# Latent attention by pairs of heads over four score banks, banded values projected features first, inner key products in 64x64 tiles

## The chip, the cores and the metric

The kernel runs on one core of one Trainium2 chip. The metric is the device time of one execution in microseconds (us). Three runs of the kernel before gave a median of 1982.02 us (1980.81 to 1982.16). The work is written out by hand for each engine: TensorE (PE, with its weight loads as PEld), VectorE (DVE), ScalarE (ACT), GpSimd (POOL) and the DMA queue of SyncE (SP), tied together with semaphores.

## What is computed

Three transformer layers over 512 tokens of width 1024, all in float32. Layer 1 ("even") has eight stick-breaking heads and eight banded heads (a window of 128 keys, two key heads), layer 2 ("mla") latent attention, layer 3 ("mix2") a linear recurrence (RWKV-7) beside differential attention. A feed-forward block follows each. The change touches these parts:

```python
# banded heads: k_b, v_b are 128 columns each of h @ w_in
# latent attention, 16 heads, 64 + 32 query/key features, 64 value features
s = (einsum('bhqd,bshd->bhqs', qn, k_nope) + einsum('bhqr,bsr->bhqs', qr, k_rope)) * 96 ** -0.5
s = where(key_pos <= q_pos, s, -inf)
p = softmax(s, axis=-1)
out = einsum('bhqs,bshd->bqhd', p, v)            # then @ w_o
# recurrence: state = state * w + (state @ -kk) (kk * a)^T + v k^T, here in chunks of 64 tokens;
# within a chunk it needs, for each head, the 64x64 products of (kk * a) with kk
```

## The kernel before

Activations lie features first: `X[:, k, :]` is 128 features by 512 tokens. A product with a weight is three products, of high and low parts (`XH`, `XL`, `w_hi`, `w_lo`) in fp32r; small products (scores, values, transposes) are plain f32, and an f32 product appears in the trace as two instructions. Weights come in units of up to 2048 columns; SP loads them, ACT makes the high part and DVE the low part (`split`), and PE waits for it (`unit`). Eight banks of PSUM hold results, and `linear`, `feature_tile` and `token_tile` (line 2365) go round banks 0 to 3.

**Banded values** (`even`, lines 2643 to 2656). After the key product of the last input unit (one `feature_tile`, line 2340, 24 products of 512 columns) PE computes the values tokens first, in four token tiles of 24 products of 128 columns each (line 2365), each waiting until DVE has emptied the bank before (line 1771). Then PE waits for the last of them (`lin_free`) and enters `stick_breaking`: `z(2)` (line 2523), then for each head `suffix(h)` (2538, 2543), `values(h-1)` (2554) and `z(h+2)`. `suffix(h)` waits for DVE's `two_parts(h)` (1668, 1670), which DVE does between the value tiles for head 1. ACT's `ln_part(h)` waits for `z(h)`.

**Latent attention** (`attention("mla0")`, `attention("mla1")`). Eight heads in each half, and 24 groups: for each head, query block 3 with 4 key tiles (512 columns), block 2 with 3 (384), and blocks 0 and 1 with 1 and 2 (384). Score banks are 0 to 2. On PE the order is `scores(n+2)` (2415, mask product 2418), `turn(n)` (2431, one transpose for each key tile), `values(n-1)` (2445: a tile of turned weights, 128x128, is stationary, and 64 value columns move past it). DVE takes the row maxima (1555) and their negation (1558), ACT the exponential with its row sum (1081) and the copy of the turned weights (1070). When a head is done, DVE normalises its output (`head_end`, 1570 and 1582) into `otok_m`, tokens first. In the second half `turn_pair` (2802, four transposes) turns two heads' output back to features first, ACT takes the high part (1295) and DVE the low part (1991). The output projection `mla_out` (2393, then 2340) starts after the eighth pair's turn.

**Inner key products** (`inner`, line 2957, within the last two units of `diff_in`). For each of four tiles `t` of two heads, ACT copies the keys of four chunks at a time as blocks of a 128x128 block-diagonal matrix (`ABD`, which DVE clears at line 2141, copies at line 1409), and PE multiplies each with 64 columns: 8 products (16 instructions) for each `t`. DVE masks the result into `Ak` (2125). PE's order is token tile 0, `inner(0)`, `inner(1)`, token tile 1, `inner(2)`, `inner(3)`, token tiles 2 and 3, and then it waits for all four (`rw_ak`). The inverse of the chunk matrices (SP, POOL) starts from `Ak` and runs beside `attention("diff")`.

```python
                for n in range(N):
                    if n + 2 < N:
                        scores(n + 2)
                    between(n)
                    turn(n)
                    if n >= 1:
                        values(n - 1)
                values(N - 1)
```

Of the kernel before, what the change touches and what calls it, by code (L numbers as in the profile page):

```python
# [8 lines left out]
F32 = mybir.dt.float32  # L9
# [4 lines left out]
ALU = mybir.AluOpType  # L14
AX = mybir.AxisListType

P = 128
# [147 lines left out]
LIN_TILES = {"even": 8 + 8 + 4 + 1 + 4 + 8, "mla": 6 + 2 * (8 + 4 + 4) + 8, "mix2": 8 + 8 + 14 + 8}  # L165


def build(nc, d, out, scratch, stages):
# [18 lines left out]
    with ExitStack() as ctx:  # L187
# [121 lines left out]
        at_p = sem("at_p")  # L309
        at_t = sem("at_t")  # L310
# [45 lines left out]
        abd_zero = sem("abd_zero")  # L356
        rw_abd = sem("rw_abd")
# [49 lines left out]
        PTb = region(2 * 512, 2, 512)  # L407
        base1 = taken[0]
# [38 lines left out]
        otok_m = region(ST * D, ST, D)  # L447
# [41 lines left out]
        ABD = NS.rearrange("p b (a c) -> p b a c", c=P)  # L489
# [76 lines left out]
        for half in range(2):  # L566
            ATT[f"mla{half}"] = dict(groups=causal_groups(), heads=8, dv=64,
                                     q=lambda h: qc[0:96, h, :], k=lambda h: kc[0:96, h, :],
                                     v=lambda h, j: vm[:, j, 64 * h:64 * h + 64], scale=96.0 ** -0.5, mask=True, q_col=True)
        ATT["diff"] = dict(groups=causal_groups(), heads=8, dv=128,  # L570
                           q=lambda h: qd[0:66, h, :], k=lambda h: kd[0:66, h, :],
                           v=lambda h, j: vd[j][:, 128 * (h // 2):128 * (h // 2) + 128], scale=0.125, mask=True, q_col=False)
        att_order = []
        for s in stages:
            att_order += {"mla": ["mla0", "mla1"], "mix2": ["diff"]}.get(s, [])
        gb = hb = 0
        for a in att_order:
            ATT[a]["g0"], ATT[a]["h0"] = gb, hb
            ATT[a]["list"] = [(h, i, tiles) for h in range(8) for i, tiles in enumerate(ATT[a]["groups"])]
            gb += len(ATT[a]["list"])  # L580
            hb += 8
        ot_base = {}
        n_ot = 0
        for s in stages:
            ot_base[s] = n_ot
            n_ot += {"even": 4, "mla": 8, "mix2": 4}.get(s, 0)

# [72 lines left out]
        def units_read():  # L660

            tiles = {"even_qkv": (2, 2, 2, 2, 4, 4), "even_qb": (0, 4), "even_kvb": (5,), "diff_in": (2, 2, 2, 2, 4, 4)}
# [29 lines left out]
        MLA_TURNS = {2: 0, 5: 1, 8: 2, 11: 3, 14: 4, 17: 5, 21: 6}  # L692
# [295 lines left out]
        def _(act):  # L988
# [55 lines left out]
            def turned_kept(k):  # L1044
                act.wait_ge(turned, 9 + k + 1)
# [13 lines left out]
            def attention(name, between=lambda n: None):  # L1059
# [12 lines left out]
                for n, (h, gi, tiles) in enumerate(groups):  # L1072
# [7 lines left out]
                    for i, k0, nk, c in tiles:  # L1080
                        last = act.activation(Pb[:, g % 3, c:c + P * nk], src[:, c:c + P * nk], ACT.Exp,
                                              bias=negm[:, hh % 2, i:i + 1],
                                              scale=qs[:, i:i + 1] if A["q_col"] else A["scale"],
# [213 lines left out]
            def mla():  # L1297
# [18 lines left out]
                for half in range(2):  # L1316
# [25 lines left out]
                    if half == 0:  # L1342
                        attention("mla0")
# [1835 lines left out]
```

## Time and profile before

| | us |
|---|---|
| median of 3 runs | 1982.02 (1980.81 to 1982.16) |
| the profiled execution | 1980.99 |
| its span, first to last instruction | 1979.0 |
| TensorE busy | 1929.9 (98%) |
| VectorE busy | 1003.2 (51%) |
| ScalarE busy | 746.1 (38%) |
| GpSimd busy | 199.8 (10%) |
| chain that ended last, by engine | PE 87%, DVE 8%, ACT 3%, issue 2% |

A TensorE row of a timeline gives the start and length of a run of like instructions. Their lengths hold the time in the pipeline, so that neighbours overlap; what an instruction costs is read from one start to the next. "Stretches" are windows of the span with each engine's busy time in them. The mean granted TensorE clock over the span is 0.993.

### The profile page before, as it was taken

Reading aid. Unit: us, or ns where it says so; the run is one execution under the profiler, and the core shown is the slowest. Engines: PE = TensorE matmul, PEld = TensorE weight load, DVE = VectorE, ACT = ScalarE, POOL = GpSimd, SP = SyncE. Lnnn points to the kernel's source line nnn. Section 1 sums busy time; section 2 is a strip of 40 time slices with the busy share of each in tenths; the row PEclk is TensorE's granted clock in tenths of the full one; section 3 lists DMA queues with packets and bytes.
Section 4 is the critical chain, followed back from the end, with each engine's and each line's share of the span. In section 5 each row is a group of like instructions: output and inputs, shape, how many; then the busy total and the mean of one; then the engine's idle time right before and its main releaser. Section 6 shows DMA issues by size and latency. Waiting matters only on the chain.

```text
span 1979.0 us, 26891 instructions
## 1 busy us (share of the span) xinstructions
PE 1929.9 (98%) x10771; PEld 1575.4 (80%) x10771; DVE 1003.2 (51%) x1349; ACT 746.1 (38%) x1116; POOL 199.8 (10%) x223
## 2 busy tenths in 40 slices
PE   8999999999999999999999999999989999999998
PEld 6886788888888777888888888777879777888887
DVE  6435644333434766543434333758573467665623
ACT  4226532222223564632222222535452444333423
POOL 3000010000000412020000000402371100000001
PEclk9999899999999999999999999999999999999999
DMA  5310022332223111023233222322120223233231
GB/s 169 107 64 1 26 87 89 102 105 86 106 85 98 58 34 64 1 88 106 85 106 95 96 99 92 98 85 64 23 65 4 92 70 105 91 100 106 86 106 64
DMA packets 137778, 158.73 MB, mean 80 GB/s; under 512 B 15960, under 2 KB 125536, under 8 KB 137696
## 3 DMA queue, kind: packets, MB, share of 16 engines
q1 hardware_dynamic: 136256, 155.01, 24.5%
q0 software_dynamic: 1440, 2.58, 0.5%
q8 instruction: 58, 0.95, 0.2%
q14 instruction: 24, 0.20, 0.0%
HBM read 153.89 MB, written 3.68 MB: 80 GB/s over the span
## 4 chain that ended last, share of the span: by engine, by line
PE 87%; DVE 8%; ACT 3%; issue 2%; DMA 0%; POOL 0%; SPq 0%; DVEq 0%; ACTq 0%; POOLq 0%
PE bank L2723 34%; PE bank L2756 16%; PE bank L2340 14%; PE bank L2365 3%; PE bank L2415 3%; PE bank L2445 3%; PE bank L2774 2%; PE bank L2431 1%; DVE XL L1532 1%; DVE w_lo L1525 1%; PE bank L2669 1%; PE bank L2702 1%; PE bank L2523 1%; PE bank L2393 1%; PE bank L2490 1%
## 5 line engine op out<-in xcount | busy, mean ns | idle before, releaser
L2723 PE MATMUL bank<-XH,w_hi 128*128 128x512 f32 x992 | 387.1, 390 | 2.6 <-DVE w_lo L1818 1.9
L2723 PE MATMUL bank<-XH,w_lo 128*128 128x512 f32 x992 | 386.1, 389 | 0.0
L2723 PE MATMUL bank<-XL,w_hi 128*128 128x512 f32 x992 | 386.1, 389 | 0.0
L2723 PEld LDWEIGHTS bank<-XH,w_hi 128*128 128x128 f32 x992 | 186.2, 188 | 42.2 <-DVE w_lo L1818 2.4
L2723 PEld LDWEIGHTS bank<-XL,w_hi 128*128 128x128 f32 x992 | 186.2, 188 | 39.3 <-issue 0.5
L2723 PEld LDWEIGHTS bank<-XH,w_lo 128*128 128x128 f32 x992 | 186.2, 188 | 38.4
L2340 PE MATMUL bank<-XH,w_hi 128*128 128x512 f32 x504 | 200.8, 398 | 4.8 <-DVE w_lo L1525 2.5
L2340 PE MATMUL bank<-XH,w_lo 128*128 128x512 f32 x504 | 197.1, 391 | 0.0
L2340 PE MATMUL bank<-XL,w_hi 128*128 128x512 f32 x504 | 196.9, 391 | 0.0
L1525 DVE TENSOR_TENSOR w_lo<-w_raw,w_hi 128x2048 fp32r<-128x2048 f32 (+4 forms) x65 | 118.1, 1835 | 91.6 <-ACT w_hi L1008 91.2
L1008 ACT ACTIVATE w_hi<-w_raw 128x2048 fp32r<-128x2048 f32 (+5 forms) x66 | 98.3, 1510 | 121.3 <-PE bank L2340 50.0
L1880 DVE TENSOR_TENSOR w_lo<-w_raw,w_hi 128x2048 fp32r<-128x2048 f32 x24 | 55.0, 2292 | 174.3 <-ACT w_hi L1268 174.3
L2756 PE MATMUL bank<-XH,w_hi 128*128 128x512 f32 x320 | 124.6, 389 | 0.0
L2756 PE MATMUL bank<-XH,w_lo 128*128 128x512 f32 x320 | 124.5, 389 | 0.0
L2756 PE MATMUL bank<-XL,w_hi 128*128 128x512 f32 x320 | 124.5, 389 | 0.0
L2340 PEld LDWEIGHTS bank<-XH,w_hi 128*128 128x128 f32 x504 | 95.0, 189 | 30.3 <-DVE w_lo L1525 4.8
L1846 DVE TENSOR_TENSOR arena<-bank,arena 128x512 f32<-128x512 f32 x66 | 45.4, 690 | 141.9 <-PE bank L2723 141.9
L1216 ACT ACTIVATE w_hi<-w_raw 128x2048 fp32r<-128x2048 f32 x32 | 61.3, 1915 | 147.5 <-PE bank L2723 147.5
L1268 ACT ACTIVATE w_hi<-w_raw 128x2048 fp32r<-128x2048 f32 x24 | 46.0, 1917 | 187.1 <-PE bank L2756 166.5
L2340 PEld LDWEIGHTS bank<-XL,w_hi 128*128 128x128 f32 x504 | 95.1, 189 | 20.8 <-issue 1.4
L2340 PEld LDWEIGHTS bank<-XH,w_lo 128*128 128x128 f32 x504 | 95.0, 188 | 19.9
L1824 DVE TENSOR_TENSOR w_lo<-w_raw,w_hi 128x2048 fp32r<-128x2048 f32 x33 | 75.6, 2290 | 62.9 <-ACT w_hi L1234 56.1
(425 smaller groups left out, 3393.6 us busy)
## 6 DMA issues: line engine op xcount, KB each, us to landing
w_raw<-in_ffn_w_gate SPq DMA_DIRECT2D x22, 1024.0 KB, 5.4
w_raw<-in_ffn_w_up SPq DMA_DIRECT2D x22, 1024.0 KB, 5.3
w_raw<-in_ffn_w_down SPq DMA_DIRECT2D x22, 1024.0 KB, 4.9
w_raw<-in_w_up SPq DMA_DIRECT2D x22, 1024.0 KB, 5.0
w_raw<-in_w_in SPq DMA_DIRECT2D x13, 1024.0 KB, 5.3
w_raw<-in_w_down SPq DMA_DIRECT2D x11, 1024.0 KB, 4.9
w_raw<-in_even_w_in SPq DMA_DIRECT2D x9, 1024.0 KB, 5.4
w_raw<-in_even_w_out SPq DMA_DIRECT2D x4, 1024.0 KB, 5.1
```

The costliest lines, as they stand in the source:

```text
L1008: last = act.activation(to, frm, ACT.Copy)
L1216: act.activation(w_hi[:, (u0 + 1) % 2, :], w_raw[:, (u0 + 1) % 2, :], ACT.Copy).then_inc(w_hi_ready, 1)
L1268: act.activation(w_hi[:, slot, :], w_raw[:, slot, :], ACT.Copy).then_inc(w_hi_ready, 1)
L1525: last = dve.tensor_tensor(to, frm, hi.bitcast(F32), ALU.subtract)
L1824: dve.tensor_tensor(w_lo[:, a, :], w_raw[:, a, :], w_hi[:, a, :].bitcast(F32), ALU.subtract).then_inc(w_lo_ready, 1)
L1880: dve.tensor_tensor(w_lo[:, slot, :], w_raw[:, slot, :], w_hi[:, slot, :].bitcast(F32), ALU.subtract).then_inc(w_lo_ready, 1)
L2340: m = pe.matmul(bank[to][0:M, :], cols(w, k), x[:, x0 + k, :], start=(first_k and k == 0 and j == 0), stop=(last_k and k == kt - 1 and j = ...
L2365: m = pe.matmul(bank[to][:, 0:N], x[:, x0 + k, s * P:(s + 1) * P], cols(w, k), start=(k == 0 and j == 0), stop=(k == kt - 1 and j == 2))
L2415: m = pe.matmul(bank[g % 3][:, c:c + P * nk], q(h)[:, P * i:P * (i + 1)], k(h)[:, P * k0:P * (k0 + nk)], start=True, stop=True)
L2445: m = pe.matmul(bank[5 + hh % 2][:, dv * i:dv * (i + 1)], PTb[:, g % 2, c + P * j:c + P * (j + 1)], v(h, k0 + j), start=(j == 0), stop=(j ...
L2723: m = pe.matmul(bank[b][:, :], w[:, k, P * c:P * (c + 1)], x[:, k, :], start=(k == 0 and j == 0), stop=(k == KT - 1 and j == 2))
L2756: m = pe.matmul(bank[p][:, :], left, right, start=False, stop=(stop and c == 1 and j == 2))
```

## The change

Three parts, in one edit.

1. The banded values become one feature tile of 24 products of 512 columns. DVE scales it into `vb` (features first), PE turns it with four transposes after `z(2)`, and DVE copies the result over `vb`. `LIN_TILES` and the counts of `turned` follow.
2. Both latent halves use a new `latent_attention`. Groups run by pairs of heads: block 3 of both, block 2 of both, blocks 0 and 1 of both. Score banks are 0, 1, 2 and 7, and scores run three groups ahead. DVE divides the exponentials by their row sums before the transpose. In the values product the 64 value columns are stationary and 128 turned weights move past, the even head into partitions 0 to 63 of the bank and the odd head into 64 to 127, so that the output comes features first; ACT and DVE make its two parts straight from there. `turn_pair` and `head_end` are gone. The first tile of `mla_out` waits for pairs 6 and 7 only where it reaches them.
3. `inner` takes for each chunk two 64x64 products, one for each head, straight from `aa`; `ABD`, its clearing and ACT's copies are gone.

```diff
@@ PE, even @@
-                for t in range(4):
-                    if t >= 1:
-                        pe.wait_ge(lin_free, L - 1)
-                    token_tile(u, KT, 256, whole(P), P, 0, t, L, to=KVB[(t + 1) % 2]).then_inc(lin_ready, 1)
-                    L += 1
-                pe.wait_ge(lin_free, L)
-                stick_breaking()
+                feature_tile(u, KT, 256, whole(P), P, 0, L, to=KVB[1]).then_inc(lin_ready, 1)
+                L += 1
+                stick_breaking(L)
+            def values_turned(L):
+                pe.wait_ge(lin_free, L)
+                for t in range(ST):
+                    m = pe.transpose(bank[KVB[0]][:, P * t:P * (t + 1)], vb[:, t, :], ident)
+                m.then_inc(turned, 1)
                 z(2)
+                values_turned(L)
@@ DVE, even @@
-                for t in range(4):
-                    dve.wait_ge(lin_ready, L + 1)
-                    dve.tensor_scalar(vb[:, t, :], bank[KVB[(t + 1) % 2]][:, 0:P], rcol[:, t:t + 1], None,
-                                      ALU.mult).then_inc(lin_free, 1)
-                    L += 1
-                    if t == 1:
-                        two_parts(1)
+                dve.wait_ge(lin_ready, L + 1)
+                dve.tensor_tensor(flat, bank[KVB[1]][:, :], rstd, ALU.mult).then_inc(lin_free, 1)
+                L += 1
+                two_parts(1)
+                dve.wait_ge(turned, 10)
+                dve.tensor_copy(flat, bank[KVB[0]][:, :]).then_inc(turned_out, 1)
@@ DVE, latent_attention @@
+                def normalised(n):
+                    dve.wait_ge(at_p, g + 1)
+                    link(dve.reciprocal(rsum[:, h % 2, i0:i1 + 1], rsum[:, h % 2, i0:i1 + 1]))
+                    for i, k0, nk, c in tiles:
+                        w = Pm[:, g % 4, c:c + P * nk]
+                        last = dve.tensor_scalar(w, w, rsum[:, h % 2, i:i + 1], None, ALU.mult)
+                    last.then_inc(at_w, 1)
+                def pair_low(p):
+                    dve.wait_ge(ot_hi, ot_base["mla"] + pp + 1)
+                    dve.tensor_tensor(lo, bank[5 + pp % 2][:, :], hi.bitcast(F32), ALU.subtract).then_inc(ot_lo, 1)
+                for n in range(len(groups)):
+                    maxima(n)
+                    if n >= 1:
+                        normalised(n - 1)
+                    if n % 6 == 5 and n >= 11:
+                        pair_low(n // 6 - 1)
+                normalised(len(groups) - 1)
+                pair_low(3)
@@ ACT, latent_attention: exp(n), then @@
+                    if n >= 2:
+                        evacuate(n - 2)
+                    if n % 6 == 4 and n >= 10:
+                        pair_high(n // 6 - 1)
@@ PE, latent_attention @@
+                def values(n):
+                    pe.wait_ge(at_pt, g + 2)
+                    if gi == 0 and pp >= 2:
+                        pe.wait_ge(ot_lo, ot_base["mla"] + pp - 1)
+                    for i, k0, nk, c in tiles:
+                        for j in range(nk):
+                            for e in range(2):
+                                m = pe.matmul(bank[5 + pp % 2][64 * e:64 * e + 64, P * i:P * (i + 1)],
+                                              vm[:, k0 + j, 64 * (h + e):64 * (h + e) + 64],
+                                              PTm[:, (g + e) % 4, c + P * j:c + P * (j + 1)],
+                                              start=(j == 0), stop=(j == nk - 1))
+                    m.then_inc(at_o, 2)
+                for n in range(N):
+                    if n + 3 < N:
+                        scores(n + 3)
+                    turn(n)          # waits for at_w, not at_p
+                    if n >= 3 and n % 2 == 1:
+                        values(n - 3)
+                values(N - 2)
@@ PE, inner @@
-                for b in range(2 * t, 2 * t + 2):
-                    pe.wait_ge(rw_abd, b + 1)
-                    for e in range(4):
-                        c = 4 * (b % 2) + e
-                        m = pe.matmul(bank[ABANK[t]][:, CH * c:CH * (c + 1)], ABD[:, b % 2, e, :],
-                                      KRk[:, t, chunk(c)], start=True, stop=True)
-                    m.then_inc(rw_a, 1)
+                pe.wait_ge(rw_keys, t + 1)
+                for c in range(NCH):
+                    for r in (side(0), side(1)):
+                        m = pe.matmul(bank[ABANK[t]][r, chunk(c)], aa[r, t, chunk(c)], KRk[r, t, chunk(c)],
+                                      start=True, stop=True)
+                m.then_inc(rw_a, 1)
```

## Rows read from the trace of the kernel before

**Rows 1.** Stretches: latent halves and stick-breaking; length, then busy us (instructions) by engine.

```profile
core 0: us, PE busy (x) PEld busy (x) DVE busy (x) ACT busy (x) POOL busy (x), PEclk, DMA share, GB/s
711.27:759.19 47.92, 47.03 (x337) 37.83 (x336) 24.30 (x74) 34.44 (x91) 0.00 (x0) 1.00 0.01 1
787.98:840.55 52.57, 50.65 (x369) 41.33 (x368) 27.81 (x80) 35.60 (x95) 0.00 (x0) 1.00 0.01 1
141.28:200.00 58.72, 57.85 (x283) 37.58 (x284) 28.21 (x45) 35.97 (x63) 0.00 (x0) 1.00 0.00 1
```

**Rows 2.** Timeline of one head of the first latent half: start, length, engine, line.

```profile
726.26 1.08 PE L2415 MATMUL bank<-arena 96*128 96x512 f32 x2
...
727.24 0.49 PE L2431 MATMUL bank<-con,arena 128*128 128x128 f32 x3
727.57 1.00 PE L2445 MATMUL bank<-arena 128*128 128x64 f32 x8
728.41 0.86 PE L2415 MATMUL bank<-arena 96*128 96x384 f32 x2
...
732.06 1.08 PE L2415 MATMUL bank<-arena 96*128 96x512 f32 x2
```

**Rows 3.** Timeline: PE's first product after the first latent half.

```profile
759.19 0.53 PE L2340 MATMUL bank<-XH,w_hi 128*128 128x512 f32 x1 [0.73 <-DVE arena L1582]
```

**Rows 4.** Timeline of the recurrence, PE: 64x64 tiles, then 128x128, then 64x64.

```profile
1490.62 0.39 PE L2977 MATMUL bank<-arena 64*64 64x128 f32 x4
1490.84 0.28 PE L2975 MATMUL bank<-arena 64*64 64x64 f32 x4
1490.95 0.39 PE L2977 MATMUL bank<-arena 64*64 64x128 f32 x4
1491.27 0.70 PE L2980 MATMUL bank<-arena,con 128*128 128x256 f32 x2
1491.90 0.51 PE L3063 MATMUL bank<-arena,under_split 64*64 64x64 f32 x10
```

**Rows 5.** Timeline of stick-breaking, PE: the values of one head, 1280 columns, 128x64 tiles.

```profile
155.24 2.37 PE L2554 MATMUL bank<-arena 128*64 128x512 f32 x8
157.53 0.70 PE L2523 MATMUL bank<-arena 128*128 128x512 f32 x1
```

**Rows 6.** Groups of instructions by form: busy us, mean ns of one.

```profile
L2554 PEld LDWEIGHTS bank<-arena 128*64 128x64 f32 x64 | 7.9, 136 | 9.4 <-issue 7.3
L1582 DVE TENSOR_TENSOR arena<-bank,small 128x256 f32<-128x256 f32 x16 | 6.8, 424 | 0.6
L1991 DVE TENSOR_TENSOR XL<-bank,XH 128x512 fp32r<-128x512 f32 x8 | 5.5, 691 | 16.3 <-ACT XH L1295 16.3
L1570 DVE RECIPROCAL small<-small 128x4 f32<-128x4 f32 x24 | 4.3, 177 | 10.2 <-PE bank L2445 10.1
L1728 DVE TENSOR_SCALAR arena<-bank,small 128x256 f32<-128x256 f32 x8 | 3.9, 482 | 12.3 <-PE bank L2365 12.3
L1977 DVE TENSOR_SCALAR arena<-arena,con 64x512 f32<-64x512 f32 x1 | 0.5, 486 | 0.0
```

**Rows 7.** Chain of work that ended last, around the banded values: start, length.

```profile
124.68 5.49 PE bank L2340 x24
130.17 10.68 PE bank L2365 x96
```

**Rows 8.** Timeline around the banded values: PE and DVE.

```profile
136.64 1.56 DVE L1670 TENSOR_TENSOR under_arena<-arena,under_arena 128x512 fp32r<-128x512 f32 x2
...
141.28 1.13 PE L2523 MATMUL bank<-arena 128*128 128x512 f32 x2 [0.44 <-DVE arena L1771]
...
143.91 1.30 PE L2543 MATMUL bank<-under_arena 128*128 128x512 f32 x6
```

**Rows 9.** Timeline around the inner products: two tiles' products, the next token tile.

```profile
1407.88 3.99 PE L2957 MATMUL bank<-arena 128*128 128x64 f32 x32
1411.68 0.36 PE L2365 MATMUL bank<-w_hi,XH 128*128 128x256 f32 x1
```

More of the change, by code:

```diff
@@ L446, in build @@
         vm = region(ST * 512, ST, 512)
-        otok_m = region(ST * D, ST, D)
+        latent_at = taken[0]
+        region(ST * D)
+        PTm = arena[:, latent_at:latent_at + 4 * 512].rearrange("p (a b) -> p a b", b=512)
+        pair_hi, pair_lo = (under_arena[:, latent_at + 2048 + 512 * i:latent_at + 2560 + 512 * i] for i in range(2))
         cq = region(5 * SEQ, 5, SEQ)
@@ L1341, in mla @@
                     L += 8
[L1342 to L1345 removed]
+                    latent_attention(half)
                 residual("mla_out", "ffn1")
@@ L2794, in ffn, with latent_out @@
                 down_unit(u0 + 10, True, ready_at(10))
-            def turn_pair(t):
-                pe.wait_ge(at_on, ATT["mla1"]["h0"] + max(2 * t - 6, 0))
-                if t >= 1:
-                    pe.wait_ge(ot_lo, ot_base["mla"] + t)
-                for i in range(ST):
-                    m = pe.transpose(bank[7][:, P * i:P * (i + 1)], otok_m[:, i, P * t:P * (t + 1)], ident)
-                m.then_inc(ot_turned, 1)
+            def latent_out(L):
+                for u in tok_units("mla_out"):
+                    unit(u)
+                    hi, lo = wv(u, 256, KT)
+                    for t in range(2):
+                        free(L)
+                        first_tile = u == first["mla_out"] and t == 0
+                        last_tile = u == tok_units("mla_out")[-1] and t == 1
+                        for n, pp in enumerate(range(KT) if first_tile else LATENT_OUT):
+                            if first_tile and pp >= 6:
+                                pe.wait_ge(ot_lo, ot_base["mla"] + pp + 1)
+                            a, b = latent_pair(pp)
+                            for j, (w, x) in enumerate(((hi, a), (hi, b), (lo, a))):
+                                m = pe.matmul(bank[L % 4][:, :], w[:, pp, P * t:P * (t + 1)], x,
+                                              start=(n == 0 and j == 0), stop=(n == KT - 1 and j == 2))
+                            if last_tile and n < KT - 1:
+                                m.then_inc(xh_free, 1)
+                        m.then_inc(lin_ready, 1)
+                        L += 1
             def mla():
@@ L2852, in mla @@
                     pe.wait_ge(krope_spread, 1)
-                    def between(n):
-                        if n == -1:
-                            pe.wait_ge(lin_free, L)
-                        if half and n in MLA_TURNS:
-                            turn_pair(MLA_TURNS[n])
-                    attention(f"mla{half}", between)
-                    if half == 0:
-                        pe.wait_ge(at_p, ATT["mla0"]["g0"] + len(ATT["mla0"]["list"]))
-                turn_pair(7)
-                linear("mla_out", L, release=True, late=("mla", {7: 8}))
+                    latent_attention(half, L)
+                latent_out(L)
             def mix2():
```

191 lines of the change are left out of this document (118 added, 73 removed).

## The prediction

> **What bounds the kernel now.** The page is read first: TensorE is busy for 98% of the span, and the chain that ended last is 87% PE. So the next question is, in each stretch that the change touches, whether PE is late or waits for somebody. The stretches answer it [rows 1]. In the first latent half PE is busy 47.03 of 47.92 us, DVE 24.30 and ACT 34.44; in the second 50.65 of 52.57; in stick-breaking after the banded values 57.85 of 58.72. PE sets the pace in all three, so time taken off PE's list comes off the span, as long as DVE and ACT keep up. The timeline of one head shows what PE's list costs [rows 2]: from one head's first score product at 726.26 to the next at 732.06 is 5.80 us. The four value tiles from 727.57 to 728.41 (8 instructions) cost 0.105 us an instruction, and the three transposes before them (727.24 to 727.57) 0.11 us each.
>
> **Latent attention, PE.** A head has 10 key tiles, so 20 value instructions: 20 x 0.105 = 2.10 us of the 5.80. Scores, masks and transposes, 3.70 us, stay as they are. Now the values move 128 columns instead of 64. An f32 product of 128 columns in a quarter of the array costs the same as its neighbour in the diagonal quarter together with it: four instructions, two products, from 1490.62 to 1490.84, 0.22 us; with 64 columns it is 0.11 us (1490.84 to 1490.95) [rows 4]. So quarters with different rows and columns run at the same time. The two halves of the new product share their 128 rows and differ in columns only, and no row shows such a pair. Lower bound: a pair costs 0.22 us, both at once. Upper bound with loads hidden: 0.44 us, one after the other. Rows 5 show that one half alone streams at full rate with its loads hidden: 1280 columns in 2.29 us, where 0.22 us for 128 makes 2.20. I take 0.22, because the nearest row in kind (two products into different partitions of one bank) is that of the quarters.
>
> Switching the array's shape costs something: after the last quarter pair at 1490.95, which needs 0.22, the 128x128 product starts 0.10 us late, and from its start at 1491.27 to the next quarters is 0.63 us where its 256 columns need 0.43, 0.20 late [rows 4]. A value block with a switch in and out is 0.30 by that, and by rows 5, where exit and all joints make 0.09, about 0.2. I take 0.25; 12 blocks a half (three for a pair of heads) make 3.0 us. Bounds are 0 and 0.30.
>
> Sum for a half: 8 x 3.70 + 40 pairs x 0.22 (10 key tiles for each of four pairs of heads) = 29.6 + 8.8 = 38.4, plus 3.0, plus start and end. At the start `turn(0)` now waits through scores, maximum, exponential, reciprocal and scaling; three more score groups (about 2.5 us) cover all but some 0.2. At the end the last group's chain leaves PE about 0.6 idle and the last values nothing behind them; PE's 0.73 wait for `head_end` [rows 3] is gone. I take 1.0 for both. That makes 42.4 against 47.92 and 52.57 [rows 1]; the second half was longer by its turned pairs, which disappear: -5.5 and -10.2, **together -15.7**.
>
> The Trainium skill, "TensorEngine Tiling (Array Packing)", Key Properties, says that changing the tiling mode drains the engine; that speaks against this change, and rows 4 agree in kind. The same section lists 128x64 as two independent tiles, which no row here shows. By that the pair costs 0.22; without it, 0.44.
>
> **Latent attention, DVE and ACT.** DVE has 24.30 / 8 = 3.04 us a head. It loses `head_end`'s product, 0.42, keeps three reciprocals for one (+0.36), and gains the scaling of 1280 columns. A scaling from SBUF to SBUF with a scalar pointer takes 0.486 us for 512 columns, one from PSUM 0.482 for 256 [rows 6]. So the scaling is between 1.2 (2.5 times the first) and 2.4 us (5 times the second); four instructions of which three are shorter than 512 make 1.5 likely, since source and destination are SBUF. `pair_low` adds 0.69 / 2 = 0.35. Sum 4.83, at most 5.73, against PE's 3.70 + 1.10 + 0.38 = 5.18. ACT in the second half, which already makes the pair copies, has 35.60 / 8 = 4.45. Both fit, and DVE only just. Scores run three groups (about 5 us) ahead of the transpose, while maximum, exponential, reciprocal and scaling with one other group between take about 3.5, so the longer chain costs nothing in the steady state. `pair_high` waits for values issued at group 6p+7 and stands at group 6p+10, so nothing queued behind it waits, except the last pair of a half: behind it are the weight splits of `mla_q1` or `mla_out`, about 1.3 us later than now. PE has four tiles of 9 products, 8.2 us at 0.229 [rows 7], before it needs them. Of the last pair's parts PE has 21 products (4.8 us) of the first `mla_out` tile as cover. Both cost nothing.
>
> **Banded values.** 96 products cost 10.68 us, 24 of 512 columns 5.49 [rows 7]: the product ends 5.2 us earlier, and the 0.44 wait before `z(2)` [rows 8] goes too, since `z(2)` no longer needs the values. `z(2)` takes 2.63 (141.28 to 143.91) and would run from 135.7 to 138.3. Four transposes add 0.44 on PE: 138.7. What is late next is DVE: `two_parts(1)` ended at 138.20 [rows 8], and now has one 0.69 evacuation before it where it had one of about 0.35, and starts later by that and by the tile's end, some 0.5: 138.8. So `suffix(1)` starts at 138.8 instead of 143.91, -5.1. ACT's `ln_part(2)` follows `z(2)` and comes 5.6 earlier, and PE was the late one in what follows [rows 1], so the gain holds. Lower bound 5.0, upper 5.6. DVE's last copy lies in its idle time before `softplus(2)`. **I take -5.2.**
>
> **Inner products.** Two tiles cost 1407.88 to 1411.68, 3.80 us [rows 9], twice. The new ones are 16 diagonal pairs of 64 columns at 0.11 [rows 4], 1.8, plus the switch in and out, 0.3: 2.1. -1.7 twice, **-3.4**. ACT's copies and DVE's clearing were off PE's path there; their removal is at most 0.2 more. `Ak` is ready earlier by as much as the attention it runs beside, so the inverse keeps its slack. Bounds -3.0 and -4.2.
>
> **Sum.** 1980.99 (the profiled execution, 1979.0 of it span) - 15.7 - 5.2 - 3.4 = **1956.7**. That execution is 1.0 us below the median, so the median would be about 1957.
>
> **Rivals.**
> A. *The halves of the array take turns.* Rows are shared, and only one moving operand enters them at a time. For it: no row shows such a pair. Against it: the quarters do overlap. Price 80 pairs x 0.22 = +17.6, so 1974. Still faster, by the other two parts.
> B. *DVE becomes the bound.* With the scaling at PSUM's price a head takes 5.73 on DVE against 5.18 on PE: 16 x 0.55 = +8.8, 1965.5. Against it: only the source in PSUM has that price in the rows.
> C. *Weight loads of the halves are not hidden.* Both halves load into rows through which the other is streaming; if a load must wait for that, each of four instructions of a pair costs its load, 0.136 [rows 6], and 0.11 of streaming, 0.98 instead of 0.22: 80 x 0.76 = +61, 2018, slower. It decides from 0.52 us a pair (0.22 + 24.3 / 80). Against it: one half alone hides its loads [rows 5].
> D. *The change does less than it says*, because chains of waits in the latent halves eat the PE time (a lead of three groups isn't enough, or ACT's exponential waits behind a copy): 0.6 us a head would return 9.6 us, 1966; it takes 1.5 a head (24.3 / 16) to return all, 1981. Against it: the 3.5 of 5 us above.
>
> **How the numbers follow.** Forecast 0.67, A 0.16, B 0.07, C 0.05, D 0.05. The forecast's own range is 1950 (no switching cost, every bound at its good end) to 1963. The range given reaches through B and A: 1950 to 1976, which leaves out C, half of D and A's far end. A measurement of this kernel can tell about 0.2% from no change, 4 us. Faster by more: forecast, B, most of A and half of D, 0.91; within: 0.04; slower: C, 0.05.
>
> **What would show it.** In the changed trace: value blocks of 12 or 16 instructions whose start-to-start time gives 0.22 or 0.44 a pair; a pair of heads at 10.4 us; PE rows of the transposes idle for DVE's scaling if B holds; DVE's scaling of 512 columns at about 0.49; `suffix(1)` some 3.3 us after the end of the value tile, 2.6 of them `z(2)`; `inner` blocks of 1.9. The prediction is wrong if value pairs cost over 0.3, if the transposes wait in steady state, or if the granted clock, 1.00 in these stretches [rows 1], falls.

## The result, and the profile after

| | before | after |
|---|---|---|
| median, us | 1982.09 (1980.81 to 1983.43, 4 runs) | 1957.32 (1955.26 to 1957.93, 4 runs) |
| the profiled execution | 1980.99 | 1957.07 |
| its span | 1979.0 | 1954.8 |
| TensorE busy | 1929.9 | 1905.8 |
| VectorE busy | 1003.2 | 1019.1 |
| ScalarE busy | 746.1 | 738.6 |

The ratio is 0.9874, with a 95% interval of 0.986 to 0.9888: 24.8 us less, where 25 were forecast.

The two latent halves, as windows of the changed kernel (length, then busy us and instructions by engine, granted clock). They answer to the first two lines of [rows 1].

```profile
core 0: us, PE busy (x) PEld busy (x) DVE busy (x) ACT busy (x) POOL busy (x), PEclk, DMA share, GB/s
704.33:746.94 42.61, 41.55 (x337) 28.58 (x335) 33.85 (x116) 33.50 (x91) 0.00 (x0) 1.00 0.01 2
775.68:818.29 42.61, 41.55 (x338) 28.59 (x336) 33.84 (x116) 33.51 (x91) 0.00 (x0) 1.00 0.00 1
```

47.92 and 52.57 have both become 42.61. VectorE works 9.6 us more in the first half and is still idle for 8.8 of 42.6.

TensorE's timeline in one block of value products, and at the end of the first half. It answers to [rows 2] and [rows 3].

```profile
722.23 0.50 PE L2529 MATMUL bank<-con,arena 128*128 128x128 f32 x3
722.65 1.09 PE L2542 MATMUL bank<-arena 128*64 128x128 f32 x16
723.68 1.12 PE L2514 MATMUL bank<-arena 96*128 96x512 f32 x2
...
745.00 0.55 PE L2529 MATMUL bank<-con,arena 128*128 128x128 f32 x3 [1.01 <-DVE arena L2022]
745.48 1.53 PE L2542 MATMUL bank<-arena 128*64 128x128 f32 x24
746.94 0.50 PE L2381 MATMUL bank<-XH,w_hi 128*128 128x512 f32 x1
```

Four steps of two products, 16 instructions, take 1.03 us from start to start; six steps, in the last line but one, take 1.46. The difference makes a step 0.215. The last three transposes of a half wait for VectorE's scaling, with TensorE idle for 1.01 us. That line also shows that the last two blocks of a half lie back to back, so that a half has 11 blocks.

TensorE and VectorE around the turned values in stick-breaking; it answers to [rows 8].

```profile
133.83 1.02 PE L2621 MATMUL bank<-arena 128*128 128x512 f32 x2
...
136.38 0.61 PE L2648 MATMUL bank<-con,arena 128*128 128x128 f32 x4
137.17 0.73 PE L2641 MATMUL bank<-under_arena 128*128 128x512 f32 x2 [0.19 <-DVE under_arena L1680]
```
```profile
134.10 0.69 DVE L1781 TENSOR_TENSOR arena<-bank,arena 128x512 f32<-128x512 f32 x1 [2.47 <-PE bank L2381]
134.71 0.82 DVE L1678 CAST under_arena<-arena 128x1280 fp32r<-128x1280 f32 x1
135.56 1.56 DVE L1680 TENSOR_TENSOR under_arena<-arena,under_arena 128x512 fp32r<-128x512 f32 x2
```

`z(2)` starts at 133.83, the four transposes at 136.38, and `suffix(1)` at 137.17, when L1680, the `two_parts(1)` of the text above, is done.

The inner products' first tiles and what follows them, against [rows 9]:

```profile
1378.73 2.08 PE L3062 MATMUL bank<-arena 64*64 64x64 f32 x64
1380.74 0.39 PE L2406 MATMUL bank<-w_hi,XH 128*128 128x256 f32 x1
```

2.01 us in place of 3.80. Summed by stages (each from one start on TensorE to another, in the two profiled executions):

| stage | before | after | difference |
|---|---|---|---|
| start to `z(0)` | 93.73 | 92.10 | -1.6 |
| `z(0)` to the first feed-forward tile | 189.31 | 184.04 | -5.3 |
| first latent half | 47.92 | 42.61 | -5.3 |
| between the halves | 28.79 | 28.74 | -0.1 |
| second latent half | 52.57 | 42.61 | -10.0 |
| first inner product to the differential attention | 17.16 | 13.73 | -3.4 |
| from there to the group norm | 127.62 | 127.54 | -0.1 |
| first of the group norm to its rows | 3.14 | 4.83 | +1.7 |

The three parts of the change are -5.3, -15.3 (two lines) and -3.4, together -24.0. The first and the last line hold no instruction that was changed; the section on the hardware comes back to them.

### The profile page after: what moved, and what is told of

It is laid out like the page before. It is cut to its first block, busy times and chain, and to the rows that moved or that the text cites. A ratio compares the mean times of both kernels' runs of the same rounds, so it can differ in the third digit from the quotient of the medians.

```text
span 1954.8 us, 26838 instructions
## 1 busy us (share of the span) xinstructions
PE 1905.8 (97%) x10735; PEld 1540.9 (79%) x10735; DVE 1019.1 (52%) x1426; ACT 738.6 (38%) x1100; POOL 199.5 (10%) x223
## 3 DMA queue, kind: packets, MB, share of 16 engines
q1 hardware_dynamic: 136256, 155.01, 24.8%
## 4 chain that ended last, share of the span: by engine, by line
PE 86%; DVE 8%; ACT 3%; issue 1%; DMA 0%; POOL 0%; SPq 0%; DVEq 0%; ACTq 0%; POOLq 0%
PE bank L2826 34%; PE bank L2859 16%; PE bank L2381 12%; PE bank L2406 3%; PE bank L2913 2%; PE bank L2514 2%; PE bank L2877 2%; DVE XL L1550 1%; DVE w_lo L1543 1%; PE bank L2772 1%; PE bank L2805 1%; PE bank L2542 1%; PE bank L2529 1%; PE bank L2456 1%; PE bank L2486 1%
## 5 line engine op out<-in xcount | busy, mean ns | idle before, releaser
L2826 PE MATMUL bank<-XH,w_hi 128*128 128x512 f32 x992 | 386.9, 390 | 2.6 <-DVE w_lo L1828 2.0
L2826 PE MATMUL bank<-XL,w_hi 128*128 128x512 f32 x992 | 386.0, 389 | 0.0
L2826 PE MATMUL bank<-XH,w_lo 128*128 128x512 f32 x992 | 385.9, 389 | 0.0
L2826 PEld LDWEIGHTS bank<-XH,w_hi 128*128 128x128 f32 x992 | 186.2, 188 | 42.2 <-DVE w_lo L1828 2.4
L2826 PEld LDWEIGHTS bank<-XL,w_hi 128*128 128x128 f32 x992 | 186.2, 188 | 39.1 <-issue 0.5
L2826 PEld LDWEIGHTS bank<-XH,w_lo 128*128 128x128 f32 x992 | 186.2, 188 | 38.8
L2381 PE MATMUL bank<-XH,w_hi 128*128 128x512 f32 x456 | 181.4, 398 | 4.1 <-DVE w_lo L1543 2.5
L2381 PE MATMUL bank<-XH,w_lo 128*128 128x512 f32 x456 | 177.7, 390 | 0.0
L2381 PE MATMUL bank<-XL,w_hi 128*128 128x512 f32 x456 | 177.5, 389 | 0.0
L2859 PE MATMUL bank<-XH,w_hi 128*128 128x512 f32 x320 | 124.5, 389 | 0.0
L2859 PE MATMUL bank<-XH,w_lo 128*128 128x512 f32 x320 | 124.5, 389 | 0.0
L2859 PE MATMUL bank<-XL,w_hi 128*128 128x512 f32 x320 | 124.5, 389 | 0.0
L2381 PEld LDWEIGHTS bank<-XH,w_hi 128*128 128x128 f32 x456 | 85.6, 188 | 27.6 <-DVE w_lo L1543 4.8
L2381 PEld LDWEIGHTS bank<-XL,w_hi 128*128 128x128 f32 x456 | 85.7, 188 | 18.6 <-issue 1.4
L2381 PEld LDWEIGHTS bank<-XH,w_lo 128*128 128x128 f32 x456 | 85.6, 188 | 18.1
```

The lines of the kernel that those rows point to most:

```text
L2381: m = pe.matmul(bank[to][0:M, :], cols(w, k), x[:, x0 + k, :], start=(first_k and k == 0 and j == 0), stop=(last_k and k == kt - 1 and j = ...
L2826: m = pe.matmul(bank[b][:, :], w[:, k, P * c:P * (c + 1)], x[:, k, :], start=(k == 0 and j == 0), stop=(k == KT - 1 and j == 2))
L2859: m = pe.matmul(bank[p][:, :], left, right, start=False, stop=(stop and c == 1 and j == 2))
```

## The experiments

Three kernels ask whether the parts are independent: the kernel before, with part 1, part 2 or part 3 of the diff alone.

**Part 1 alone, the banded values.**

> The kernel before with the banded-values part alone (values projected features first, turned by four products in the stick-breaking stage). Theory: -5.2 us against the kernel before, all between the first scores and the first feed-forward stage, 5.1 of it in the head that held the old projection; 1976.9. Rival (the parts are not additive, a stall that one part removes is filled by another): a saving that differs from 5.2 by over 1 us. Second question: whether the group norm's variance products, which took 4.8 us in place of 3.1 in the changed kernel, stay at 3.1 here; if they are lengthened by where the stage falls in time rather than by the inner products, they may be longer here too, and the saving is 3.5.

1976.43 us, ratio 0.9969 (0.9958 to 0.998), so 6.1 less than before. From `z(0)` to the first feed-forward tile: 182.55. In the run of part 3 alone, where that stage has the code of before and the same granted clock, it is 187.87. (The clock has two levels, 1.2 and 2.4 GHz; a figure between 0.5 and 1 is the mean over a window, as a share of the higher. It is 0.79 in both runs over the 16 us in which it falls in this stage, against 0.68 in before and after.) That makes -5.3 for the part, and 1.4 for the clock. The group norm's stretch is 3.14, but the clock falls 100 us behind it; the section on the hardware has the line.

**Part 2 alone, the latent attention.**

> The kernel before with the latent attention by pairs of heads alone. Theory: -15.4 us (5.3 in the first half, 10.0 in the second), 1966.7, each half 42.6 us long. Rival (the parts are not additive): the halves differ from 42.6 by over 0.5 us, or the whole saves another sum than the two halves do. If the lowered clock in the group norm belongs to the parts before or after, it is absent here.

1965.02 us, ratio 0.9915 (0.9899 to 0.9932). Both halves:

```profile
709.92:752.53 42.61, 41.55 (x337) 28.59 (x335) 33.85 (x116) 33.51 (x91) 0.00 (x0) 1.00 0.01 2
781.27:823.88 42.61, 41.54 (x337) 28.58 (x335) 33.85 (x116) 33.51 (x91) 0.00 (x0) 1.00 0.01 2
```

These are the changed kernel's halves to 0.01 us. The group norm's stretch is 3.14.

**Part 3 alone, the inner products.**

> The kernel before with the inner key products in 64x64 tiles alone. Theory: -3.4 us (two stretches of 3.8 us become 2.1 each), 1978.7; if the lowered clock in the group norm comes with this part, +1.7 of it is given back and the saving is 1.7, 1980.4. Rival (the copies of key blocks that ScalarE no longer makes also shorten the stage): over -4.

1976.22 us, ratio 0.9978 (0.9967 to 0.9989). The stage takes 13.74 in place of 17.16, -3.4, and the group norm 3.14. So the rival, over -4, doesn't hold for the stage. By their stages the parts are additive to 0.1 us. Their totals, 6.1 + 16.8 + 4.4 = 27.3 by the ratios, are not a sharp test: each has an interval of 2 us or more to either side. The lower clock in the group norm came with no single part.

Four kernels ask what made the value products cheap.

**Head by head.** The products of a block in another order:

```diff
-                        for j in range(nk):
-                            for e in range(2):
+                        for e in range(2):
+                            for j in range(nk):
                                 m = pe.matmul(bank[5 + pp % 2][64 * e:64 * e + 64, P * i:P * (i + 1)],
```

> The changed kernel with the value products of a block ordered head by head, so that successive products lie in the same half of the array; same products, same shapes, same waits. Theory (two products in different halves run side by side, 0.22 us for the two; in the same half one after the other): 80 steps of two products, each 0.22 longer, +17.6 us, 1974.9. Rival 1 (the short products never overlapped and are cheap because only 64 columns are loaded): no change, 1957.3. Rival 2 (products are bound by their issue or by the weight loads, which still overlap): under +6 us.

1962.96 us, ratio 0.9906 (0.9889 to 0.9922). A half takes 45.30, so 2.69 more and not 8.8. TensorE's timeline in a block of four steps:

```profile
723.54 1.58 PE L2542 MATMUL bank<-arena 128*64 128x128 f32 x16
725.05 1.12 PE L2514 MATMUL bank<-arena 96*128 96x512 f32 x2
```

1.51 us in place of 1.03. The starts of the single instructions explain it. Within one head they lie 0.109 us apart. But at 724.03, 0.006 behind the first head's fifth, one starts that is 0.323 us long, as only the first of a head is. The records don't name the head, but by lengths and spacing this is the second head's first, while the first head's last three are still to come (724.13, 724.24, 724.35), and from there the two run interleaved. So the order of issue does not put the halves in turn: instructions for the other half overtake those that wait. The theory's price was for products that cannot overlap, and here some 4 of each head's 8 instructions still did. By its total, 5.6 us more than the changed kernel, the run fits rival 2 (under +6), so it left open whether halves in turn have a price of their own.

**Both heads in one half.** Nothing can overlap (the upper half of the output isn't computed):

```diff
-                                m = pe.matmul(bank[5 + pp % 2][64 * e:64 * e + 64, P * i:P * (i + 1)],
+                                m = pe.matmul(bank[5 + pp % 2][0:64, P * i:P * (i + 1)],
...
-                                              start=(j == 0), stop=(j == nk - 1))
+                                              start=(j == 0 and e == 0), stop=(j == nk - 1 and e == 1))
```

> The changed kernel with both heads' value products in the lower half of the array, so that the upper half of the output isn't computed (left out: the odd head's own place; the products are as many and as long). Ordering head by head gave only +2.5 us per half of the attention, since the two halves' queues still overlapped at the change of head. Here nothing can overlap. Theory (a step of two products takes 0.218 side by side, 0.436 in one half): 40 steps of 0.218 more, each half of the attention 42.6 + 8.7 = 51.3 us, the whole 1974.8. Rival (products of 64 columns are cheap by themselves): 45.1 per half at most, 1962.

```profile
703.65:754.05 50.40, 50.20 (x337) 37.27 (x336) 33.85 (x116) 33.62 (x91) 0.00 (x0) 1.00 0.01 1
```

1973.32 us, ratio 0.9957 (0.9943 to 0.997). A half takes 50.40: 42.61 + 40 x 0.218 = 51.33. At the end the last transposes start 0.36 late in place of 1.23, since TensorE is slower; less that 0.87 it is 50.46. Within a block the instructions lie 0.109 apart, but for the second, 0.16 behind the first. A block of 16 takes 1.89, so the order head by head, at 1.51, had saved 0.38 by overtaking, three or four instructions. So a product costs 0.218 in one half, and two in different halves cost the same together.

**The whole array.** As in the changed kernel, but each product takes all 128 columns, so that the shape never changes:

```diff
-                                m = pe.matmul(bank[5 + pp % 2][64 * e:64 * e + 64, P * i:P * (i + 1)],
-                                              vm[:, k0 + j, 64 * (h + e):64 * (h + e) + 64],
+                                m = pe.matmul(bank[5 + pp % 2][:, P * i:P * (i + 1)],
+                                              vm[:, k0 + j, 64 * h:64 * h + 128],
```

> The changed kernel with each value product over all 128 columns of the array, two in turn in place of the pair side by side (left out: the separation of the two heads in the result), so that no shape changes. Theory: each step 0.218 longer as in one half, but the changes of shape go, each 0.09 (0.20 between the last product of one shape and the first of the other in place of 0.11): 12 blocks with two changes, -2.2 per half of the attention: 42.6 + 8.7 - 2.2 = 49.1 us, the whole 1970.4. Rival (a change of shape costs nothing, the 0.09 is a wait): 51.3 as in the run with both heads in one half.

```profile
706.13:753.53 47.40, 46.95 (x338) 37.71 (x336) 33.85 (x116) 33.62 (x91) 0.00 (x0) 1.00 0.01 1
```

1967.55 us, ratio 0.9923 (0.9901 to 0.9945). A half takes 47.40, which is 3.00 less than with both heads in one half. In the steady state a pair of heads, three blocks, takes 11.59 here and 12.50 there, 0.30 a block. The price is more than the 0.18 that I expected, and 0.30 is still too little, because a product's instructions lie 0.112 apart over the whole array and 0.109 in a half, 0.10 for a pair of heads. Start by start, the run with both heads in one half differs in four places around a block: the first instruction starts 0.09 late, the second 0.05, the next score product 0.09, and the instruction behind that one 0.10, together 0.33. I had counted the first and the third, in the changed kernel's trace.

The run shows one thing more. Its 80 products move 128 columns over the whole array, those of the kernel before moved 64, and a half took 47.92 there. The instructions of before lie 0.111 to 0.112 apart too, but for the second of a block (0.06), in the blocks of [rows 2]. So in the kernel before, moving half the columns saved next to nothing, and swapping the operands alone gains 0.5 us in the first half. In the second it also does away with the turned pairs, which had made that half 52.57. All the rest of the gain is that two products run side by side. Why 64 columns took as long as 128 there was not tried.

**One block for a pair of heads.** Ten steps in one block, for three of the four pairs of a half:

```diff
-        PTm = arena[:, latent_at:latent_at + 4 * 512].rearrange("p (a b) -> p a b", b=512)
+        PTm = arena[:, latent_at:latent_at + 8 * 512].rearrange("p (a b) -> p a b", b=512)
...
-                    if n >= 3 and n % 2 == 1:
-                        values(n - 3)
-                values(N - 2)
+                    if n % 6 == 1 and n > 6:
+                        values(n - 7, 3)
+                    if n in (N - 3, N - 1):
+                        values(n - 3, 1)
+                values(N - 2, 1)
```

> The changed kernel with the value products of a pair of heads in one block of ten steps in place of three blocks, for three of the four pairs of a half (eight buffers for the turned scores in place of four; the last pair as before). Same products. Theory: 6 blocks fewer in each half, each with two changes of shape of 0.09 us: 1.1 less per half, 41.5 us, the whole -2.2, 1955.1. Rival (a block of 2.3 us starves ScalarE and VectorE of scores and turned tiles, and TensorE waits after it): the same or longer, waits of 0.2 to 1 us after each block.

1957.62 us, ratio 0.9874 (0.985 to 0.9898). A half takes 42.60: nothing gained. The timeline between two such blocks:

```profile
726.46 0.22 PE L2516 MATMUL bank<-masks,identB 128*128 128x128 bf16 x1
726.76 0.55 PE L2529 MATMUL bank<-con,arena 128*128 128x128 f32 x3
...
727.79 0.22 PE L2516 MATMUL bank<-masks,identB 128*128 128x128 bf16 x1
728.14 0.65 PE L2529 MATMUL bank<-con,arena 128*128 128x128 f32 x4
...
730.00 2.40 PE L2543 MATMUL bank<-arena 128*64 128x128 f32 x40
```

A transpose normally starts 0.06 us after the mask product; here it is 0.30 and 0.35, and the transpose behind each is 0.05 late as well, 0.63 together. From one such block to the next it is 10.29 us, 0.06 less than a pair of heads took, so that two blocks fewer had saved 0.69. TensorE reads 40.77 us busy in place of 41.55. So the rival won, and the next three runs bear on what these waits are.

**Two multiplies.** VectorE's scaling is followed by a multiply by one:

```diff
-                        last = dve.tensor_scalar(w, w, rsum[:, h % 2, i:i + 1], None, ALU.mult)
+                        link(dve.tensor_scalar(w, w, rsum[:, h % 2, i:i + 1], None, ALU.mult))
+                        last = dve.tensor_scalar(w, w, 1.0, None, ALU.mult)
```

> The changed kernel with the scaling by the row sums followed by a second multiply by one, the same shapes, on VectorE. VectorE is busy 33.85 of the 42.6 us of a half; the second multiply adds 32 of 0.42 on average less the fixed part, some 12 us, so VectorE would be busy 46 us. Theory (VectorE has 1.1 us of slack per head, no more): it becomes the bound, a half takes 47 to 49, the whole 1966 to 1970. Rival (VectorE's work is hidden whatever it is, since three groups of scores are ahead): the half stays within 1 us of 42.6.

```profile
705.09:753.60 48.51, 43.74 (x337) 28.53 (x335) 43.14 (x148) 33.12 (x91) 0.00 (x0) 1.00 0.01 1
782.33:832.21 49.88, 45.10 (x338) 29.68 (x336) 43.15 (x148) 33.12 (x91) 0.00 (x0) 0.97 0.00 1
```

1972.09 us, ratio 0.9953 (0.9934 to 0.9971). VectorE works 9.3 us more and a half takes 5.9 more (7.3 where the clock was lowered). The first half is within the forecast (47 to 49); the whole, 1972.1, is above it (1966 to 1970), and so is the second half. TensorE waits for VectorE's scaling in 9 places, 4.5 us: VectorE's chain sets the pace here, at 5.4 busy us for 6.1 of a head. It was close: of VectorE's 9.3 us more, 3.4 cost nothing.

**One block and no scaling.** The kernel with one block for a pair, without VectorE's scaling:

```diff
-                    link(dve.reciprocal(rsum[:, h % 2, i0:i1 + 1], rsum[:, h % 2, i0:i1 + 1]))
-                    for i, k0, nk, c in tiles:
-                        w = Pm[:, g % 4, c:c + P * nk]
-                        last = dve.tensor_scalar(w, w, rsum[:, h % 2, i:i + 1], None, ALU.mult)
-                    last.then_inc(at_w, 1)
+                    dve.reciprocal(rsum[:, h % 2, i0:i1 + 1], rsum[:, h % 2, i0:i1 + 1]).then_inc(at_w, 1)
```

> The kernel with one block of ten steps, and VectorE's scaling of the scores left out (only the reciprocal stays, so that the weights are not divided by their sums). Theory (in that kernel the waits are VectorE's): 6 blocks fewer at 0.34 (-2.0), and the waits for the scaling at the half's end and start go (1.0 and 0.3): 42.6 - 3.3 = 39.3 us per half, the whole 1950.7. Rival (joining the blocks gains nothing, the waits have another cause): 41.3, only the end and the start are gained.

```profile
702.95:742.89 39.94, 39.24 (x337) 28.54 (x336) 23.38 (x84) 31.54 (x91) 0.00 (x0) 1.00 0.01 2
```

1951.60 us, ratio 0.9852 (0.9821 to 0.9884). A half takes 39.94, between 39.3 and the rival's 41.3. The 0.6 above my sum is a new wait, the last transposes' for ScalarE's copy:

```profile
engine line waited for: us in total, times, longest us
PE bank L2525 <- ACT arena L1105: 0.7, 1, 0.7
```

With it, 6 x 0.34 + 1.0 + 0.3 - 0.7 = 2.6 of the 2.67 found. From block to block it is 9.66 us, where the changed kernel takes 10.35 for a pair of heads: 0.69 = 2 x 0.34. Laid beside the kernel with the scaling, from one block to the next, each step from start to start is the same within 0.012 us but four: those to the two late transposes and to the two behind them. So joining the blocks does gain its 0.34 each once VectorE has time: the waits in the kernel above were VectorE's. That the scaling's removal alone, without joined blocks, gives 41.3 was not run.

**Two blocks for a pair of heads.** Four steps, then six, with six buffers:

```diff
+                    if n % 6 == 3 or n == N - 1:
+                        values(n - 3, 1)
+                    if n % 6 == 1 and n > 6:
+                        values(n - 5, 2)
+                values(N - 2, 1)
```

> The changed kernel with the second and third block of value products of a pair of heads joined, so that two blocks (four steps, six steps) stand in place of three, for three of the four pairs of a half (six buffers in place of four). In the kernel with one block of ten steps a change of shape showed a price of 0.34 us per block (0.09 before it, 0.05 within, 0.09 and 0.10 behind it), but what it saved went into later turnings, which came 0.3 us late. Theory (that was VectorE falling behind in the stretch without value products, which is shorter here): 3 blocks fewer per half, -1.0 each half, 41.6 us, the whole 1955.3. Rival (VectorE sets the pace however the blocks lie): 42.6 as before.

```profile
704.41:746.00 41.59, 40.52 (x338) 28.57 (x336) 33.34 (x116) 33.50 (x91) 0.00 (x0) 1.00 0.01 2
774.72:816.31 41.59, 40.52 (x338) 28.58 (x336) 33.34 (x116) 33.49 (x91) 0.00 (x0) 1.00 0.00 1
```

Each half takes 41.59, 1.02 less, 0.34 for each of the three blocks saved, to the hundredth. The total, 1955.59 us, ratio 0.9876 (0.9851 to 0.9902), can't be told from the changed kernel's: 1.7 us are 0.1%. By its stages it is the best kernel here of those that leave nothing out.

**A lead of two groups.**

```diff
                 scores(1)
-                scores(2)
                 for n in range(N):
-                    if n + 3 < N:
-                        scores(n + 3)
+                    if n + 2 < N:
+                        scores(n + 2)
```

> The changed kernel with the scores issued two groups ahead of the turning instead of three. From the end of a group's scores to its turning the chain maximum, exponential, sum, reciprocal, scaling takes 2.7 us at the start of a half (705.3 to 708.0 us of the changed kernel's trace), where nothing else is queued. Two groups ahead, TensorE has 2.1 us of other work in that time where no block of value products lies between, 2.9 to 3.6 where one does. Theory (the third group is what hides the chain): waits of 0.3 to 0.6 us at the turning of most groups, a half 46 to 50 us, the whole 1964 to 1972. Rival (the chain is hidden with two groups already, the third is only room): a half stays within 1 us of 42.6.

```profile
702.74:751.61 48.87, 43.93 (x337) 28.49 (x336) 34.18 (x116) 32.96 (x91) 0.00 (x0) 1.00 0.01 1
```
```profile
engine line waited for: us in total, times, longest us
PE bank L2529 <- DVE arena L2022: 4.9, 11, 1.2
```

1968.39 us, ratio 0.9938 (0.9917 to 0.9958). A half takes 48.87, 6.3 more, while VectorE's busy time is the same within 0.3. TensorE is idle for VectorE's scaling in 11 places, 4.9 us. So the third group of the lead is what hides the longer chain, and it is worth 12.5 us by the two halves (11.1 by the medians), about half of what the change gained.

**Inner products side by side.** All eight chunks of the upper rows, then of the lower ones:

```diff
-                for c in range(NCH):
-                    for r in (side(0), side(1)):
+                for r in (side(0), side(1)):
+                    for c in range(NCH):
```

> The changed kernel with the inner key products ordered side by side: the eight chunks of the upper rows first, then the eight of the lower ones. Same products and shapes. Theory (as in the run ordered head by head: a quarter takes a pass every 0.058 us, and only some four passes overlap at each change of quarter): four runs of 16 passes, 3.7 us less three overlaps of 0.23, 3.0 us in place of 2.1 in each of the two stretches, from the inner products to the differential attention 15.6 in place of 13.7 us, the whole 1959.2. Rival (the products are bound by their issue, whatever quarter they lie in): 13.7, no change.

```profile
1378.29 3.40 PE L3062 MATMUL bank<-arena 64*64 64x64 f32 x64
1381.62 0.39 PE L2406 MATMUL bank<-w_hi,XH 128*128 128x256 f32 x1
```

1960.77 us, ratio 0.9904 (0.9878 to 0.9931). 3.33 us in place of 2.01, twice; the stage takes 16.36 in place of 13.73. So the order has its price, and the products are not bound by their issue. The overlap at a change of quarter is smaller than I took (4 x 16 x 0.058 = 3.7, less 0.4, not 0.7). With that, 1.3 of the 1.8 us that a stretch gained over the kernel before hang on the order of the loops.

## Why the prediction was right, point by point

**Latent attention.** -15.7 forecast, -15.3 measured; 42.4 against 42.61 for a half. The working held in the large and less well in its terms:

- The pair of products: 0.22 taken, 0.215 to 0.218 measured. This was the disputed step, and both bounds are now shown: side by side 0.218 (the changed kernel), in one half 0.436. Rival A's price was right (8.8 of a half by 40 x 0.22, 8.7 by the products in one half), and its condition doesn't hold. Rival C's condition doesn't either: loads are hidden.
- The change of shape: 0.25 a block taken, 0.34 measured by the run with two blocks and 0.33 start by start. The sum had 12 blocks, and the kernel has 11, since the last two lie back to back: 3.7 in place of 3.0. The bound of 0.30 was too low; [rows 4] show the first product after the switch late, and not what follows the switch into the smaller shape.
- Scores, masks and transposes: 3.70 taken. A pair of heads takes 10.35 (713.33 to 723.68), and less 10 steps of 0.218 and 3 blocks of 0.34 that is 7.15, 3.58 a head. The 0.12 too much belonged to the values of before: behind each of their three blocks a head, the second score instruction came 0.05 later than behind transposes (0.485, 0.378 and 0.165 in place of 0.433, 0.322 and 0.11), and it was counted with the scores. The 0.12 are 1.0 for a half, and hid the errors beside it.
- Start and end, 1.0 for both: 1.5 measured. At the end TensorE is idle for 1.01, and counted by starts the last transposes come 1.23 late. At the start `turn(0)` begins at 708.04, 0.28 behind the last mask product where 0.06 is usual, and it comes 0.27 late in all.
- Together: 8 x 3.58 + 8.7 + 3.7 + 1.5 = 42.6. The errors are -1.0, +0.7, +0.5 and -0.1.

**VectorE.** 4.83 a head taken, 33.85 / 8 = 4.23 measured. The scaling is as forecast: 0.486 us for 512 columns, and 11.7 / 8 = 1.46 a head where 1.5 was taken. The 0.6 is in how I added: durations of single instructions were put on top of a busy time in which overlapping ends count once. The durations of VectorE's 116 instructions of a half add up to 38.2 us, 4.78 a head, and the busy time is 33.85. Rival B didn't happen, but the reasoning that "both fit, VectorE only just" was on the right side. The two multiplies and the joined blocks show the room left: 3.4 us of a half in the one, none in the other, since what counts there is the stretch between two blocks and not the mean.

**The lead.** That the longer chain costs nothing in the steady state held: between the first and the last transposes of a half, none starts over 0.07 us behind the mask product before it. Nor did the last pair's two parts cost anything: between the halves it is 28.74 for 28.79. With two groups it costs 6.3 us a half. Rival D is this mechanism; it was given 0.05, and the design is one group away from it.

**Banded values.** -5.2 forecast, -5.3 measured. Its inner step is right as well: `z(1)` began at 119.05 before and at 117.42 after, so all of this stage lies 1.6 earlier; the forecast had `suffix(1)` 138.8 - 119.05 = 19.75 after it, and it starts 137.17 - 117.42 = 19.75 after it. It waits for `two_parts(1)`, as forecast, not for the transposes.

**Inner products.** -3.4 forecast, -3.4 measured: 2.01 us a stretch where 2.1 was taken.

**The sum.** Of the span, -24.2 (1979.0 to 1954.8) against -24.3. Some of this closeness is luck. In each half the error of -1.0 us cancels +0.7 and +0.5, and outside the changed parts -1.6 at the start and +1.7 in the group norm cancel, which the forecast did not have.

## What to carry to other kernels

Two f32 products that use different halves of the array's columns and share its rows cost one, but only where they are issued alternately; put the loop over halves innermost. Each excursion into another shape costs some 0.34 us here, so join blocks, but spread them so that the engine that feeds the next step keeps up between two of them. When a step is added to a chain between two uses of TensorE, count how many groups of work are issued ahead before you count the chain's engines: here the third group was worth half the gain.

## What the runs showed of the hardware

**Instructions for different halves overtake.** An instruction for a free half starts while three issued earlier still wait for the other half (724.03 against 724.13 to 724.35, head by head, read by lengths and spacing). A block of 16 took 1.51 us where one half alone took 1.89. That is why the order cost 2.7 us a half and not 8.7.

**The granted clock moves between stretches from run to run.** TensorE's clock falls to its lower level in a few short stretches of each execution, and they lie elsewhere after a change in another stage. The same two parts of the program, before and after: the start (12 us) and the group norm (8 us).

```profile
8.00:20.00 12.00, 9.53 (x44) 7.24 (x43) 6.95 (x9) 6.67 (x9) 3.47 (x3) 0.86 0.95 284
1544.00:1552.00 8.00, 6.09 (x20) 3.71 (x21) 3.39 (x5) 4.30 (x8) 0.00 (x0) 1.00 0.40 131
```
```profile
8.00:20.00 12.00, 10.02 (x51) 7.12 (x49) 8.57 (x10) 6.67 (x9) 4.95 (x4) 1.00 1.12 309
1518.00:1526.00 8.00, 6.00 (x12) 2.85 (x13) 1.91 (x2) 2.54 (x5) 0.00 (x0) 0.79 0.40 131
```

With the start at 0.86 `z(0)` came 1.6 us later; with the group norm at 0.79 its stretch took 4.83 in place of 3.14. The first varies between executions: with the same code up to there, `z(0)` starts at 92.5 to 94.3 us in the seven kernels whose start reads 0.86, and at 91.2 to 92.7 in the seven with 1.00. So how much of the 1.6 is the clock's isn't shown.

The second is steadier. It is 4.83 in the changed kernel and in eight of its nine variants, and 3.14 before and with each part alone. In the ninth variant, the one without scaling, it is 3.14 too. But there, and with part 1 alone, the clock falls 100 us later, and what lies behind the group norm takes 1.6 us more than in the other kernels. Part 1 alone, then the kernel without scaling:

```profile
1637.00:1645.00 8.00, 6.26 (x20) 5.04 (x21) 7.15 (x8) 3.32 (x3) 0.00 (x0) 0.79 0.41 134
1612.00:1620.00 8.00, 6.45 (x21) 5.17 (x22) 7.15 (x8) 3.32 (x3) 0.00 (x0) 0.79 0.41 133
```

So each of the eleven kernels with part 1 loses 1.6 to 1.7 us in one of these two places, and the three without it (before, part 2 alone, part 3 alone) in neither. What in part 1 leads to it wasn't tried and stays open; one trace of each kernel is all there is. Nor does every such stretch cost time: in the recurrence the clock reads 0.83 before and 0.91 after over 20 us, and the time from the differential attention to the group norm is 127.62 and 127.54.
